# Norms of a transformer block's first projection: squares folded on VectorE, inverse roots repeated over partitions by DMA

## The reference

```python
h = ada_norm(x, norm1_g, sh1, sc1)
proj = h @ w_in                     # q 256, k 256, v 256, c_q 384, c_kv 256, k_rope 32, conv 768
q = rms_norm(q.reshape(b, t, 4, 64), na_q_g)    # per head of 64
k = rms_norm(k.reshape(b, t, 4, 64), na_k_g)
y_na = neighbourhood_attention(q, k, v, na_rpb)
# latent attention begins with
rms_norm(c_q, q_a_g) @ w_uq         # over 384
rms_norm(c_kv, kv_a_g) @ w_ukv      # over 256
k_r = apply_rope(rms_norm(k_rope, kr_g), cos, sin)   # over 32
```

## Time and profile before

| | |
|---|---|
| three timed runs | 3150.15 us median, 3148.28 to 3152.46 |
| the profiled execution | 3145.51 us, its span 3143.9 us |
| busy share of the span | TensorE 94%, weight loads 74%, VectorE 55%, ScalarE 32%, POOL 13% |
| chain that ended last | TensorE 79%, VectorE 11%, issue 4%, ScalarE 3%, DMA 2% |
| units 7 to 17 of the projection | 149.1 to 298.6 us |

### The profile page before, as it was taken

One profiled execution on the slowest core, in us unless ns is written; L12 is line 12 of the kernel. 1 busy time (PEld: TensorE's weight loads), 2 busy tenths in 40 slices (PEclk: granted clock), 3 DMA queues, 4 the chain that ended last, 5 costly groups with the idle time before them and its releaser, 6 DMA issues.

```text
span 3143.9 us, 40427 instructions
## 1 busy us (share of the span) xinstructions
PE 2966.0 (94%) x16581; PEld 2317.6 (74%) x16581; DVE 1729.3 (55%) x1883; ACT 1010.0 (32%) x1309; POOL 420.9 (13%) x461
## 2 busy tenths in 40 slices
PE   2998999999999999999998999999979999999989
PEld 2886666667788888888777887878767886666667
DVE  5534635663445545543495747557454226676784
ACT  2122535552211111111233424225232114444452
POOL 0002010000111111100101102021111001333340
PEclk7999999999999999999999999999978999999999
DMA  6334110010133333321114233242311322212121
GB/s 228 116 112 113 24 31 17 20 28 28 54 101 113 118 116 100 113 87 48 41 54 123 82 88 107 67 127 81 99 62 34 107 81 67 68 34 63 39 73 62
DMA packets 244027, 245.89 MB, mean 78 GB/s; under 512 B 13317, under 2 KB 207714, under 8 KB 243874
## 3 DMA queue, kind: packets, MB, share of 16 engines
q1 hardware_dynamic: 220160, 167.07, 17.6%
q0 software_dynamic: 17680, 58.89, 6.3%
q10 hardware_dynamic: 6034, 17.74, 1.4%
HBM read 214.89 MB, written 26.40 MB: 77 GB/s over the span
## 4 chain that ended last, share of the span: by engine, by line
PE 79%; DVE 11%; issue 4%; ACT 3%; DMA 2%; ACTq 0%; SPq 0%; POOL 0%; DVEq 0%; POOLq 0%
PE PU L942 16%; PE PU L944 16%; PE PU L943 16%; PE PM L1601 2%; PE PU L1579 2%; PE PU L1271 2%; DVE small L2709 2%; PE PM L1589 2%; PE PM L1621 2%; PE PM L1623 2%; DMA seg<-decay_sums 2%; PE PM L1622 2%; PE PU L956 1%; PE PU L1202 1%; PE PU L957 1%
## 5 line engine op out<-in xcount | busy, mean ns | idle before, releaser
L942 PE MATMUL PU<-hH,w_hi_t 128*128 128x512 f32 (+1 forms) x1872 | 740.0, 395 | 2.4 <-DVE w_lo_t L2327 2.4
L944 PE MATMUL PU<-hH,w_lo_t 128*128 128x512 f32 (+1 forms) x1872 | 731.2, 391 | 0.0
L943 PE MATMUL PU<-hL,w_hi_t 128*128 128x512 f32 (+1 forms) x1872 | 730.4, 390 | 0.0
L2327 DVE TENSOR_TENSOR w_lo_t<-w_raw,w_hi_t 128x1024 fp32r<-128x1024 f32 x181 | 228.1, 1261 | 433.3 <-ACT w_hi_t L1733 421.2
L942 PEld LDWEIGHTS PU<-hH,w_hi_t 128*128 128x128 f32 (+1 forms) x1872 | 351.6, 188 | 77.5 <-DVE w_lo_t L2327 3.8
L944 PEld LDWEIGHTS PU<-hH,w_lo_t 128*128 128x128 f32 (+1 forms) x1872 | 351.1, 188 | 76.2
L943 PEld LDWEIGHTS PU<-hL,w_hi_t 128*128 128x128 f32 (+1 forms) x1872 | 351.6, 188 | 72.0
L1733 ACT ACTIVATE w_hi_t<-w_raw 128x1024 fp32r<-128x1024 f32 x167 | 174.6, 1045 | 457.4 <-PE PU L944 356.4
L2777 DVE SCALAR_TENSOR_TENSOR xT<-PU,mod,xT 128x1024 f32<-128x1024 f32 x120 | 154.0, 1284 | 201.0 <-PE PU L944 201.0
L3057 DVE TENSOR_TENSOR_SCAN s_keep<-s_keep,zero 128x128 f32<-128x128 f32 (+7 forms) x128 | 180.6, 1411 | 2.0 <-POOL s_keep L897 2.0
L897 POOL TENSOR_SCALAR_AFFINE_SELECT s_keep<-s_keep 128x128 f32<-128x128 f32 x128 | 114.4, 910 | 501.5 <-ACT s_keep L2215 500.9
(11 more groups left out here) (420 smaller groups left out, 5026.4 us busy)
## 6 DMA issues: line engine op xcount, KB each, us to landing
ada_w<-in_ada_w_dram POOLq DMA_DIRECT2D x64, 384.0 KB, 4.1
w_raw<-in_w_gu_dram SPq DMA_DIRECT2D x44, 512.0 KB, 3.7
w_raw<-in_m_in_w_dram SPq DMA_DIRECT2D x40, 512.0 KB, 3.8
ada_w<-in_w_ada_dram POOLq DMA_DIRECT2D x32, 512.0 KB, 4.5
seg<-decay_sums SPq DMA_DIRECT2D x32, 512.0 KB, 4.3
w_raw<-in_w_down_dram SPq DMA_DIRECT2D x22, 512.0 KB, 3.3
w_raw<-in_w_in_dram SPq DMA_DIRECT2D x17, 512.0 KB, 3.8
ada_w<-in_w_ada_dram SPq DMA_DIRECT2D x16, 512.0 KB, 19.4
```

Of the source, the lines that this page charges most:

```text
L942: mm(PU[0:width, up, half, :], whi, aH[:, k, cols], start=k == 0, stop=False)
L943: mm(PU[0:width, up, half, :], whi, aL[:, k, cols], start=False, stop=False)
L944: last = mm(PU[0:width, up, half, :], wlo, aH[:, k, cols], start=False, stop=k == kt - 1)
L2327: V.tensor_tensor(w_lo_t[:, p, 0:w], w_raw[:, p, 0:w], w_hi_t[:, p, 0:w].bitcast(F32), ALU.subtract)\
```

## The change

Seven norms (q0, q1, k0, k1, cq, ckv, krope; `NORMS`) from ten units (`FOLDS`) get another path.

- VectorE takes the squares first: `squares_folded` transposes `j_sq` in 32x32 blocks into half of `ada_acc1` and reduces it to `h_red`, 32 numbers in each partition. It stands ahead of `split` in the iteration behind the unit.
- TensorE adds what is left over partitions: `norm_sums` multiplies `h_red` (32 columns) by `fold` or `fold64`, one product for a unit: 1 each for q0, q1, k0 and k1, 3 for cq, 2 for ckv, none for krope. `column_sums`, `head_spread`, the two calls of `spread` in this loop and the repeat for krope are gone.
- The root is over 128x32. VectorE takes the reciprocal, turns it in 32x32 blocks to `g_turned`, and SP's `norm_rows` stores it as rows of `scr_n` (two stores of 4 KB for q and k, one else), waits for that, and reads the rows back repeated over the partitions into `n_bc` in SBUF (two loads of 256 KB, or one of 512 KB; 128 KB for krope). It stands behind the panel of four units later.
- `norm_applied` waits for `g_land` and reads `n_bc`. The first product of neighbourhood attention no longer waits for krope's sums behind it in TensorE's order.

```diff
+            def norm_rows(e):                                  # SP
+                kind, _ = NORMS[e]
+                n = NORM_ROWS[e]
+                r0 = 64 if kind == "krope" else 0
+                sp.wait_ge(g_turn, e + 1)
+                for r in range(n):
+                    sp.dma_start(scr_n[r, :].rearrange("(j c) -> j c", c=32), g_turned[r0 + HD * r:r0 + HD * r + 32, 0, :]).then_inc(g_store, 16)
+                sp.wait_ge(g_store, 16 * sum(NORM_ROWS[:e + 1]))
+                if e:
+                    sp.wait_ge(j_done, e)
+                rows = 32 if kind == "krope" else P // n
+                for r in range(n):
+                    sp.dma_start(n_bc[r0 + rows * r:r0 + rows * (r + 1), :], scr_n[r:r + 1, :].broadcast_to([rows, T])).then_inc(g_land, 16)
...
-            for kind, t, c0 in WIN_UNITS:
+            for n, (kind, t, c0) in enumerate(WIN_UNITS):
                 panel(...)
+                if n >= 4 and WIN_UNITS[n - 4][0] in ("q", "k"):
+                    norm_rows(NORMS.index(WIN_UNITS[n - 4][0:2]))
             for t in range(2):
                 panel(w_out[:, :, t * P:(t + 1) * P], KD, P)
+                norm_rows(4 + t)
+            norm_rows(6)
...
-            def column_sums(rhs, bank=0, rows=P, r0=0, first=True, final=True):
-                pe.wait_ge(sq_ready, sq.next())
-                if first and normed.n:
-                    pe.wait_ge(j_done, normed())
-                for t in range(TT):
-                    last = mm(PM[:, bank, w * t:w * t + w], j_sq[r0:r0 + rows, t * P:(t + 1) * P], rhs, ...)
+            def norm_sums(e):                                  # TensorE, in the middle of the next unit
+                pe.wait_ge(sq_fold, slots[-1] + 1)
+                roots_read()
+                sel = fold64 if kind in ("q", "k") else fold
+                for n, f in enumerate(slots):
+                    last = mm(PM[:, 0, 0:32], sel[:, :], h_red[:, f % 4, :], start=n == 0, stop=n == len(slots) - 1)
                 last.then_inc(stat_done, 1)
-            def head_spread():
-                pe.wait_ge(c_inv, cr.next())
-                for t in range(TT):
-                    for hd in range(2):
-                        last = mm(PM[hd * HD:(hd + 1) * HD, t // 4, ...], rt[:, 0, ...].broadcast_to([P, HD]), ident[:, :], ...)
...
-            column_sums(blk96[64:96, 64:65], bank=0, rows=ROPE, r0=64)
...
-            pe.wait_ge(c_inv, cr.next())                       # krope, ahead of the head units
-            for t in range(TT):
-                last = mm(PM[64:96, ...], rt[:, 1, t:t + 1].broadcast_to([P, ROPE]), ident[:, :], ...)
...
+            def norm_root(e):                                  # ScalarE
+                if e:
+                    act.wait_ge(g_turn, e)
+                if kind == "krope":
+                    act.wait_ge(sq_fold, len(FOLDS))
+                    src = h_red[64:96, (len(FOLDS) - 1) % 4, :]
+                    ins = af(n_rt[64:96, :], src, ACT.Sqrt, bias=EPS, scale=1 / ROPE)
+                else:
+                    act.wait_ge(stat_done, e + 1)
+                    ins = af(n_rt[:, :], PM[:, 0, 0:32], ACT.Sqrt, bias=EPS, scale={"cq": 1 / QR, "ckv": 1 / KVR}.get(kind, 1.0))
+                ins.then_inc(c_root, 1)
...
+            def squares_folded(f):                             # VectorE
+                ve.wait_ge(sq_ready, f + 1)
+                link(V.transpose(ada_acc1[r, 1, :], j_sq[r, :]))
+                V.tensor_reduce(h_red[r, f % 4, :], ada_acc1[r, 1, :].rearrange("p (j b) -> p j b", b=32), AX.X, ALU.add).then_inc(sq_fold, 1)
+            def norm_inverse(e):
+                ve.wait_ge(c_root, cr.next())
+                link(V.reciprocal(n_rt[r, :], n_rt[r, :]))
+                if e:
+                    ve.wait_ge(g_store, 16 * sum(NORM_ROWS[:e]))
+                V.transpose(g_turned[r, 0, :], n_rt[r, :]).then_inc(g_turn, 1)
             for n, (kind, t, c0) in enumerate(WIN_UNITS):
+                if n and WIN_UNITS[n - 1][0:2] in NORM_UNITS:
+                    squares_folded(FOLDS.index(WIN_UNITS[n - 1][0:2]))
                 if n:
                     split()
...
-            norm_applied("ckv", 1)
-            inverse_columns(TT, b=1)
+            squares_folded(len(FOLDS) - 1)
+            norm_applied(NORMS.index(("ckv", 1)))
+            norm_inverse(len(NORMS) - 1)
```

More of the change, by code:

```diff
@@ L151 @@
 ADA_AT_UNIT = (6, 10, 14, 17)
+NORM_UNITS = {(kind, t): n for n, (kind, t, _) in enumerate(WIN_UNITS) if kind in ("q", "k", "cq", "ckv", "krope")}
+FOLDS = list(NORM_UNITS)
+NORMS = [("q", 0), ("q", 1), ("k", 0), ("k", 1), ("cq", 2), ("ckv", 1), ("krope", 0)]
+NORM_ROWS = [2 if kind in ("q", "k") else 1 for kind, _ in NORMS]
 HEAD_TILES = [("qr", t) for t in range(MH // 4)] + [("qn", t) for t in range(MH // 2)] + [("kn", t) for t in range(MH // 2)]
@@ L1101, in _ @@
                     feat_unit(wp, 0, P, KD, hH, hL, mid=mid)
-                prior, pt_, _ = WIN_UNITS[n - 1]
-                if prior in ("q", "k"):
-                    head_spread()
-                    normed.next()
-                if (prior, pt_) in (("cq", 2), ("ckv", 1)):
-                    spread(rt[:, 0, :])
-                    normed.next()
-                if kind in ("q", "k"):
-                    later.append(lambda: column_sums(blk64[:, 0:P:HD]))
                 if kind == "v":
                     later.append(lambda t=t: values_transposed(t))
-                if kind == "cq":
-                    if t == 0:
+                if (kind, t) in NORMS and kind != "krope":
+                    if kind == "cq":
                         later.append(lambda: pe.wait_ge(nv_tok, 2))
-                    later.append(lambda t=t: column_sums(ones[:, 0:1], first=t == 0, final=t == 2))
-                if kind == "ckv":
-                    later.append(lambda t=t: column_sums(ones[:, 0:1], first=t == 0, final=t == 1))
+                    later.append(lambda e=NORMS.index((kind, t)): norm_sums(e))
                 if n in ADA_AT_UNIT:
                     ada_columns()
-            column_sums(blk96[64:96, 64:65], bank=0, rows=ROPE, r0=64)
             def na_scores(s):
@@ L1186, in _ @@
             pe.wait_ge(na_o, NA_STEPS)
-            pe.wait_ge(j_done, normed())
-            pe.wait_ge(c_inv, cr.next())
-            for t in range(TT):
-                last = mm(PM[64:96, t // 4, (t % 4) * P:(t % 4 + 1) * P], rt[:, 1, t:t + 1].broadcast_to([P, ROPE]), ident[:, :],
-                          start=True, stop=True)
-            last.then_inc(c_bc, 1)
-            normed.next()
+            pe.wait_ge(j_done, NORMS.index(("ckv", 1)) + 1)
             def head_unit(n):
@@ L2365, in ada_slab @@
                     ada_reduced(acc, turned, job.n % 2)
+                    reduced.next()
             def ada_finish(parts):
@@ L2378, in _ @@
             hh = Tally()
[L2380 removed]
+            cr, bc = Tally(), Tally()
             def model_inverse():
@@ L2643, in _ @@
             cr.next(HEAD_UNITS)
+            bc.next(HEAD_UNITS)
             skip(HEAD_UNITS - 2)
@@ L2665, in mix_inverse @@
                     return
-                if r:
-                    ve.wait_ge(g_store, 64 * (r + 1))
+                ve.wait_ge(g_store, 16 * sum(NORM_ROWS) + (64 * (r + 1) if r else 0))
                 ve.wait_ge(g_done, r + 1)
@@ L2673, in mix_apply @@
             def mix_apply(j):
-                ve.wait_ge(g_land, 32 * (j + 1))
+                ve.wait_ge(g_land, 16 * sum(NORM_ROWS) + 32 * (j + 1))
                 y = y_tile(MIX_ORDER[j])
```

112 lines of the change are left out of this document (63 added, 49 removed).

## The result

The changed kernel takes 3122.46 us (median of 4 runs, 3118.97 to 3125.96) where the kernel before, beside it, takes 3149.68 (3148.28 to 3152.46): ratio 0.9918, 95% interval 0.9905 to 0.993. Forecast were 3125.3 us in a range of 3119 to 3137. The profiled execution took 3125.96 us (span 3124.3) and is the slowest of the four; against before's 3145.51 it saves 19.6 us, the medians 27.2. Timed once more later, the same kernel gave 3125.88 (3122.16 to 3131.42, 6 runs) and a ratio of 0.993 [0.9918, 0.9942]. So the saving is 20 to 30 us, and one profile can't say more than that of the whole; the times of single stages can be read to a tenth.

What follows compares the result with a forecast made beforehand. TensorE's own work bounds units 6 to 17, the bias tables the start behind unit 17. 26.9 + 1.9 - 2.9 - 1.0 = 24.9 us off the median 3150.15 gives 3125.3 us, range 3119 to 3137.

Steps and rivals of the forecast that it cites:

- What goes and what TensorE gets, in the stage: Units 7 to 17: removing TensorE's sums and spreads saves 26.9 us, the new fold products cost 2.9.
- 2.9 for the fold products: TensorE's nine new products in six groups, 18 records, cost 2.9 us; bounds 0.6 and 5.0.
- krope's repeat: TensorE's repeat ahead of the head units, after neighbourhood attention: removal worth 1.9 us; bounds 0 and 1.9.
- The fold is hidden, with 1.8 us to spare: VectorE's ten folds, 24.7 us, cost 0: ready at 3.6 us of a unit, wanted by TensorE at mid-unit, 5.4.
- The exchange is hidden: SP's row stores (1.4 us) and repeated loads (3.8) land 2.9 us into the next unit; VectorE asks at 4.8.
- the second reserve: In the sign-turned rival: late rows stop TensorE only when over 1.9 + 1.8 and odd idle us, say 5 us late.
- the slower exchange: Rival: stores and loads wait for slabs in flight, round trip some 12.5 us, 12.9 us lost, 3138; chance 0.16.
- The end of the stage: Behind unit 17: tables at T + 8.7 against T + 8.53, `pos` loading sooner; 1.0 us lost, bounds 0 and 3.
- No change: Rival: gain given back at neighbourhood attention's start, bias tables some 20 us late, or never reaching the end; 3148; chance 0.05.
- sign turned: Rival: exchange round trips beyond 15.6 us make the kernel slower; at 20 us, 3176; chance 0.06.
- the small products are free: Rival: TensorE's fold groups cost 0.6 us and `pos` no delay, 28.2 us saved, 3122; inside the range, no separate chance.
- signs of being wrong: TensorE waiting for `h_red` or a low part in the stage, or the span after unit 17 growing over 3 us.

Runs made afterwards that it cites:

- slabs held back: Changed kernel, POOL's next slab held until row stores land, or until repeated rows land: 3123.35 us (ratio 0.9926) and 3123.77 us (0.9927).
- the filler: Changed kernel plus twelve idle TensorE products behind the first scores of neighbourhood attention, results unused: 3118.76 us, ratio 0.9912.
- the doubled fold: Changed kernel with VectorE transposing and reducing every unit's squares two times: 3132.98 us, ratio 0.9958.
- ckv first: Changed kernel with VectorE applying ckv's norm ahead of folding krope's squares instead of behind it: 3124.77 us, ratio 0.9924.
- the exchange twice: Changed kernel with SP storing and loading each set of rows, waiting for landing, then doing it again: 3147.05 us, ratio 1.0002.

## Why the prediction was right

The forecast of 3125.3 us held, and so did its main steps. Some of the closeness is luck. The sum was 24.9 us off the profiled execution, and the profiled executions differ by only 19.6, the medians by 27.2, and by 22.5 when timed again. Stage by stage, the profile has 24.4 for units 7 to 17, then loses 0.4 up to the tables and 0.75 up to the head units, where 1.9 were to be gained, 1.3 before unit 7 and 2.3 behind the first latent scores, two parts on which the forecast had put nothing. There the profiles of these kernels differ by 2.4 and 10.4 us.

- **What goes and what TensorE gets, in the stage.** 24.0 us forecast, 24.39 measured. Put back by themselves, sums and spreads cost 16.27 and 10.06 us, 26.3 together, where the removed were taken at 26.9. The step "2.9 for the fold products" was a little too high: a single group costs 11.15 - 10.87 = 0.28 us (0.36 had been taken), ckv's two products 11.44 - 10.87 = 0.57.
- **krope's repeat.** It stood there for 1.91 us and is gone. Without it the kernel before would stand at 70.6 - 1.9 = 68.7 from tables to head units, and the changed kernel with its slabs held back does, at 68.8 and 68.7. The changed kernel itself stands at 71.3 in both of its profiles, and its variants, whose attention steps are the same but for the filler, at 67.6 to 70.8: it loses 2.6 us in the longer stretches at half clock shown above, and so the 1.9 doesn't appear in its own profile.
- **The fold is hidden, with 1.8 us to spare.** Shown by the doubled fold, which overdraws it at once; by it the cover is 1.5 to 1.9 us.
- **The exchange is hidden.** Right in the sum, wrong in the reason. The step that failed is that VectorE "waits for nothing, with 1.9 us to spare": stores landed after 3.5 us by the median where 1.4 was taken, the loads after 4.0, and VectorE waited up to 3.79 us. The round trip for k1 is 9.5 us, from the store's issue at 192.94 to 202.45, where 6.4 was taken. (The estimate of 2.0 and 3.2 us by the Trainium skill's fit, "DMA: Bandwidth & Descriptors", section "Anatomy of one DMA", falls short as the rows did: 5.2 against the measured 3.5 + 4.0, which decide.) What saved the forecast is the second reserve, which it had kept for the rival alone: a late landing reaches TensorE only through the next fold, past VectorE's own idle time (36.1 us ahead of eight folds by the view of waits, 7.34 ahead of the first) and the 1.8. So the slower exchange came true in its mechanism, at no cost. Its size was about half of the 12.5 us of the rival, but that number was too high for its own terms: with 4.5 us for the store and 4.5 for the loads the sum gives 10.2. And the 4.6 us that the rival took for the latest store belong to a load; the stores of the earlier trace rows landed after 3.1 us at most, by the view of the tile `g_turned`. The rival also charged each late row in full, without the reserve. Twice over, the exchange costs 18.7 us of the stage, which makes the sign a matter of one more exchange.
- **The rule of the Trainium skill** ("DMA: Bandwidth & Descriptors", section "Queues, rings and completion order"), that a semaphore's increment lands only after earlier writes of the same DMA engine across its queues, was given as what could bring that rival. These runs agree with its direction: a store is down when the slab issued ahead of it is (161.36 against 161.2 us), and 2.0 us after its issue once the slab is held back. They don't settle whether the increment waits by that rule or the 4 KB merely stand in line behind the slab's bytes.
- **The end of the stage.** 1.0 us taken, 0.42 measured, and the cause named first, `pos`, was not it: `pos` starts at T + 4.7, and the tables are there before VectorE is, for in the changed kernel it goes from ckv through the reciprocal to line 2571 without a wait. VectorE's order is the bound, as the doubled fold (+2.52) and ckv first (a wait of 1.21 us again) show.
- **Rivals.** No change and sign turned did not come. That the small products are free did not either: they cost 0.28 each.

One of the prediction's own signs of being wrong did come: the span after unit 17 was to grow by no more than 3 us, and it grew by 3.5, from 2845.3 to 2848.8, in both profiles of the changed kernel. The danger named for it, a longer stretch at half clock behind the gap, is there: with 1.27 us of work behind unit 17 the clock granted there is 0.72 where it was 0.79, it stays at 0.50 for 1.5 us longer behind the tables, and falls once more for 6.8 us instead of 3.4. That costs 2.6 us, of which krope's 1.9 give back the most; 0.4 lie ahead of the tables and 2.3 behind the first latent scores. The filler holds the clock at 1.00 across the gap, and the three timings with it are the three lowest; where each of their us lies isn't settled, since the last column of the table, 2674 to 2684 us, moves by more than the filler is worth. It goes partly with the granted clock over the whole: one kernel, the changed one timed again, took 3131.42 us at 0.968 and 3125.36 at 0.973.

## What to carry to other kernels

Where one engine is busy for all of a stage, take small products off it even if VectorE must work about as long in their place (24.7 us of folds for the 24.4 saved in the stage), and price them by the pitch of units with and without them. For everything that the change puts on other engines, work out two reserves, the time at which the result is asked for and the idle time between that wait and the engine that bounds: a store that landed 2.5 times as late as planned cost nothing because of the second. And price a small DMA by what is in flight beside it at its place, not by a row from a quieter stretch.

## What was not expected of the hardware

- From the issue of the first 4 KB store to the loads that wait for it, 1.38 us passed with no slab in flight and 3.5 to 4.3 with one of 512 KB issued just before on another queue; with the slabs held behind the stores it was 1.4 to 2.2.
- Behind unit 17 TensorE has 1.27 us of work where it had 5.12, and the granted clock of the stretch is 0.72 where it was 0.79; a filler of twelve products kept it at 1.00, in a kernel whose gap was long enough for them. It fell to 0.50 for 6.8 us later on all the same.
- Around one and the same wait of TensorE of 2.09 us in neighbourhood attention the granted clock fell to 0.50 for 6.8 us in both profiles of the changed kernel, and for 3.4 us in the kernel before and in the two with slabs held back.
- Executions of one kernel differ by up to 15 us (3140.6 to 3155.26 for the exchange twice), with mean granted clocks of 0.971 and 0.966: stages read from the trace to a tenth of a us tell more here than the median of the whole.
